# Adding the two expert sums into the residual: reloads and VectorE additions, or accumulating transfers issued by GpSimd

## What is computed

```python
    # hier_moe: every token goes to its two best experts
    y = jax.ops.segment_sum(y_buf[dest] * w_s[:, None].astype(h.dtype), tok_s, num_segments=n_tok)

    # first_block
        x = x + hier_moe(h, ...)
    return rmsnorm(x, norm_final)

    # second_block
    h = layer_norm(x, ln_in_g, ln_in_b)
    for l in range(DEPTH_2):
        proj = jnp.einsum('bsd,de->bse', h, w_in[l])
        ...
```

## Time and profile before

| | us |
|---|---|
| median of three runs | 2050.75 |
| lowest, highest | 2048.8, 2050.97 |
| the profiled execution, its own time | 2045.53 |
| span of its trace, first to last instruction | 2044.3 |
| of it: last expert product on TensorE ends | 757.5 |
| first product of the next layer starts | 801.3 |

### The profile page before, as it was taken

How to read it: one execution, slowest core, us unless ns; L and a number is a source line. 1 busy time by engine, 2 the same in 40 slices (tenths; PEclk the granted TensorE clock), 3 DMA queues, 4 the chain that set the end, 5 groups by cost and what they waited for, 6 DMA issues and landing times.

```text
span 2044.3 us, 26578 instructions
## 1 busy us (share of the span) xinstructions
PE 1842.1 (90%) x10396; PEld 1453.1 (71%) x10396; DVE 958.1 (47%) x1881; ACT 777.7 (38%) x1436; POOL 394.9 (19%) x438
## 2 busy tenths in 40 slices
PE   6999999986998762999899999998999899999997
PEld 5888776765554432876778888787876778888785
DVE  4358776554211015778445333233777445333234
ACT  3245476211333234566352232214566253232221
POOL 1019154102222211134002111000133002111001
PEclk9999999997999995998999999999998999999999
DMA  4334300474999983211222333232211222333231
GB/s 145 88 105 125 102 2 2 165 281 194 371 383 401 393 325 115 72 54 51 82 93 90 105 94 96 90 100 66 81 63 42 83 93 88 105 97 94 90 95 52
DMA packets 134884, 264.43 MB, mean 129 GB/s; under 512 B 11616, under 2 KB 92128, under 8 KB 122464
## 3 DMA queue, kind: packets, MB, share of 16 engines
q1 hardware_dynamic: 116320, 228.35, 32.6%
q10 hardware_dynamic: 13312, 25.90, 3.7%
q0 software_dynamic: 5120, 8.40, 1.3%
HBM read 254.22 MB, written 16.78 MB: 133 GB/s over the span
## 4 chain that ended last, share of the span: by engine, by line
PE 52%; DMA 9%; DVE 8%; ACT 3%; issue 2%; POOL 1%; PEld 1%; PEldq 0%; ACTq 0%; POOLq 0%; SPq 0%; DVEq 0%
PE b L507 15%; PE b L508 14%; PE b L509 14%; DMA m<-in_w_gate_up 6%; PE b L1987 3%; ACT m L620 2%; DVE m L2695 2%; DMA m<-in_w_down 1%; PE b L2520 1%; PE b L2012 1%; PE b L2502 1%; PE b L2488 1%; ACT m L688 1%; DVE m L692 1%; DMA s_h<-m 1%
## 5 line engine op out<-in xcount | busy, mean ns | idle before, releaser
L507 PE MATMUL b<-m,m 128*128 128x512 f32 (+3 forms) x2060 | 783.8, 380 | 62.6 <-DVE m L493 21.9
L509 PE MATMUL b<-m,m 128*128 128x512 f32 (+3 forms) x2060 | 773.9, 376 | 0.0
L508 PE MATMUL b<-m,m 128*128 128x512 f32 (+3 forms) x2060 | 773.8, 376 | 0.0
L493 DVE TENSOR_TENSOR m<-m,m 128x1024 fp32r<-128x1024 f32 (+1 forms) x212 | 278.3, 1319 | 514.3 <-ACT m L483 513.9
L507 PEld LDWEIGHTS b<-m,m 128*128 128x128 f32 x2060 | 394.1, 191 | 141.6 <-issue 36.9
L509 PEld LDWEIGHTS b<-m,m 128*128 128x128 f32 x2060 | 393.7, 191 | 67.1
L508 PEld LDWEIGHTS b<-m,m 128*128 128x128 f32 x2060 | 394.5, 191 | 64.1
L483 ACT ACTIVATE m<-m 128x1024 fp32r<-128x1024 f32 (+1 forms) x236 | 245.8, 1048 | 500.3 <-PE b L509 472.4
L2945 POOL TENSOR_TENSOR m<-m,m 128x512 fp32r<-128x512 f32 x44 | 71.1, 1636 | 422.1 <-ACT m L2891 422.1
L1987 PE MATMUL b<-m,m 128*64 128x256 f32 x1024 | 126.5, 390 | 26.9 <-DMA m<-in_w_gate_up 25.2
L1987 PEld LDWEIGHTS b<-m,m 128*64 128x64 f32 x1024 | 73.5, 139 | 78.2 <-issue 38.2
(11 more groups left out here) (339 smaller groups left out, 1895.8 us busy)
## 6 DMA issues: line engine op xcount, KB each, us to landing
m<-in_w_gate_up SPq DMA_DIRECT2D x64, 1024.0 KB
m<-in_w_gu SPq DMA_DIRECT2D x88, 512.0 KB, 3.6
m<-in_w_down SPq DMA_DIRECT2D x32, 1024.0 KB
m<-in_w_in SPq DMA_DIRECT2D x48, 512.0 KB, 3.8
m<-in_w_down SPq DMA_DIRECT2D x44, 512.0 KB, 3.7
m<-in_w_in SPq DMA_DIRECT2D x20, 448.0 KB, 3.6
m<-in_w_o SPq DMA_DIRECT2D x16, 512.0 KB, 4.0
s_gt<-m ACTq DMA_DIRECT2D x16, 256.0 KB, 2.0
```

The lines of the kernel that those rows point to most:

```text
L493: e.tensor_tensor(flat(wlo[HX[i]], i), flat(raw[RX[i][0]], i), fr(flat(whi[HX[i]], i)), ALU.subtract).then_inc(sem("w_lo"), 1)
L507: e.matmul(out, xh, yh, start=start, stop=False, skip_group_check=True)
L508: e.matmul(out, xh, yl, start=False, stop=False, skip_group_check=True)
L509: return e.matmul(out, xl, yh, start=False, stop=stop, skip_group_check=True)
```

## The change

The eight reloads and VectorE's eight additions go. GpSimd issues eight transfers that add into `X1` in SBUF: first those of the first half of `Y2` for the four tiles. For each tile it then waits until that one has landed (`yb` at 16), and issues the one of the second half. VectorE's multiplication and ScalarE's squares wait for `yb` at 32, both sums added. GpSimd's four roots stand behind the eight transfers. The other lines only place semaphore counts anew.

```diff
         def sync_final(e):
             e.wait_ge(*at("over", 1))
-            for t in range(NT):
-                e.dma_start(YA[2 * t + 1], Y2[S + t * P:S + t * P + P, :]).then_inc(sem(f"ya{2 * t + 1}"), 16)
...
         def scalar_final(e):
             e.drain().then_inc(sem("over"), 1)
-            for t in range(NT):
-                e.dma_start(YA[2 * t], Y2[t * P:t * P + P, :]).then_inc(sem(f"ya{2 * t}"), 16)
...
-                    e.wait_ge(*at("f_sum", i + 1))
+                    e.wait_ge(*at(f"yb{i}", 32))
                     e.wait_ge(*at("rms_sq", SQUARES[2] + i))
...
         def vector_final(e):
             for i in range(7):
                 if i < 4:
-                    x, y = YA[2 * i], YA[2 * i + 1]
-                    e.wait_ge(*at(f"ya{2 * i}", 16))
-                    e.wait_ge(*at(f"ya{2 * i + 1}", 16))
-                    e.tensor_tensor(x, x, y, ALU.add).then_inc(sem("f_pair"), 1)
-                    e.wait_ge(*at("f_pair", i + 1))
-                    e.tensor_tensor(X1[:, i, :], X1[:, i, :], x, ALU.add).then_inc(sem("f_sum"), 1)
+                    y = YA[2 * i + 1]
...
-                    e.wait_ge(*at("f_sum", i + 1))
+                    e.wait_ge(*at(f"yb{i}", 32))
...
         def gpsimd_final(e):
+            for t in range(NT):
+                e.dma_start(X1[:, t, :], Y2[t * P:t * P + P, :], accum_op=ALU.add).then_inc(sem(f"yb{t}"), 16)
+            for t in range(NT):
+                e.wait_ge(*at(f"yb{t}", 16))
+                e.dma_start(X1[:, t, :], Y2[S + t * P:S + t * P + P, :], accum_op=ALU.add).then_inc(sem(f"yb{t}"), 16)
             for t in range(NT):
                 ln_root(e, 0, t)
```

## The result

| | before | changed |
|---|---|---|
| median of the timed executions, us | 2050.97 (7; 2048.8 to 2056.06) | 2063.02 (7; 2055.49 to 2065.46) |
| ratio, with its 95% interval | | 1.0047 [1.0029, 1.0066] |
| that is, in us | | +9.6 (5.9 to 13.5) |
| the profiled execution, its own time | 2045.53 | 2063.7 |
| span of its trace | 2044.3 | 2062.5 |

The ratio is estimated from all executions of both kernels, whose means (2051.86 and 2061.58) are 9.7 us apart; the medians are 12.1 apart. The changed kernel is slower by 0.47%. The two traces lie 18.2 us apart, nearly twice the 9.6 us. So the first thing to do is to split them at two marks in code that the change leaves alone: the issue of the last scatter, and the first product. Between them lies the stage, 8.3 us longer. The other 9.9 us lie outside: 5.1 ahead of the last scatter and 4.8 behind the first product.

A forecast was written before the change was run, and what follows sets the result against it. Bound: the chain of waits from last scatter to TensorE's first product. A0 = 773.45 + 4.0 + 5 x 2.68 = 790.9, product at 810.4 instead of 801.26; 2050.75 + 9.1 = 2059.9 us, range 2048 to 2070.

The forecast's parts named there:

- A0: Time at which tile 0 holds both sums; forecast at 790.9 us, where the kernel before has 777.66.
- fixed part: GpSimd's transfers, issue to data flow: 2.35 us as for reloads plus 1.0 for GpSimd's own issue, 3.35 us.
- release: Last scatter's landing to GpSimd's first issue, past the branch: ScalarE's 2.78 us assumed, issue at 770.1.
- the weights ahead of A0: SyncE's next three weight chunks, 1.57 MB at 390 GB/s, put wholly ahead of tile 0's sums: 4.0 us.
- The gain: VectorE's dropped additions bring TensorE's first product to A0 + 19.5 in place of + 23.6: 4.1 us.
- Two passes per tile: Accumulating transfers read SBUF as well as DRAM: 2.68 us a tile, first product 9.1 us later; chance 0.45.
- One pass: Rival on accumulating transfers: second read overlaps the first, 1.34 us a tile, 2.4 us later, 2053.2; chance 0.20.
- the third pass: Rival on accumulating transfers: software queue's factor 1.5 too, 4.0 us a tile, 17.3 us later, 2068; three or more 0.22.
- The weights give way: Rival on SyncE's weights: they fall behind the sums; at one pass 1.6 us earlier, 2049.2; chance 0.08.
- The roots: Rival: transfers out of order make tile 0's root on GpSimd wait for the last issue; costs its lateness; no chance given.
- Faster: Rival: GpSimd leaves the branch without the 2.78 us, plain tile speed, ahead of weights; 4.5 us earlier, 2046.2; chance 0.05.
- From the product on: TensorE's first product to the end: same 1243.0 us as before; a change by some us would mean being wrong.

The follow-up runs named there:

- plain_hold: The changed kernel with its eight transfers made plain (sums left out) and SyncE's next weights held back until all have landed; stage 40.37 us, no ratio timed.
- hold: The changed kernel with SyncE's next weights held back until all eight sums are in; ratio to the kernel before 1.0024.
- order: The changed kernel with GpSimd's eight transfers issued in another order, tile 0's second sum fourth instead of fifth; ratio to the kernel before 1.0076.
- after_again: The changed kernel once more, unedited, under a new name; ratio to the kernel before 1.0046.
- early: The kernel before with all eight reloads issued by SyncE once the scatters have landed, without waiting for the branch; ratio to the kernel before 1.0007.
- hybrid: The kernel before with second sums added by GpSimd's transfers, first sums still reloaded by ScalarE and added by VectorE; ratio to the kernel before 1.0019.

## Why the prediction was right, point by point

It forecast 2059.9 us in a range of 2048 to 2070, slower with 0.64. The changed kernel takes 2063.02. The forecast was a shift of 9.1 us from the median of before; the two timed comparisons give 9.6 and 9.4. In the traces the way from the first issue to A0 was 0.8 us shorter than laid out. In that sum the tiles were 0.7 us too dear and the fixed part 0.6, while the weights were 0.55 too cheap, so part of the closeness is errors that cancel.

| step | predicted | measured |
|---|---|---|
| release: last scatter's landing to the first issue | 2.78 | 3.32 |
| fixed part of a chain of GpSimd's transfers | 3.35 | 2.7 accumulating (15.44 - 5 x 2.54), 3.6 plain (9.99 - 5 x 1.27) |
| the weights ahead of A0 | 4.0 | 4.55, alone 4.21 |
| one accumulating tile | 2.68 | 2.54 |
| first issue to A0 | 20.75 | 19.99 |
| A0 to the first product | 19.5 | 19.28 |
| period, with a wait for the root | 3.77, 0.66 | 3.81, 0.69 |
| the stage | + 9.1 | + 8.3, + 8.5 |

- **The gain** of 4.1 us came: 23.60 - 19.28 = 4.3. The layout by hand of three programs from the earlier trace rows was off by 0.2 us in 19.5, and that is its rounding: A0 + 8.8 with 3.3, 1.05 and 1.15 us makes + 14.3, not + 14.4, and 0.1 us was put on top. Kernels with four different A0 have 19.26 to 19.28 here.
- **Two passes per tile** was the step that decided. Its price held (2.54 us for 2.68); that the second read is what it pays for is not shown. One pass falls with `plain_hold` against `hold` (1.27 and 2.54), and so does the third pass: the factor of 1.5 of the software queue in the earlier trace rows doesn't hold for whole tiles. To take the row of another access pattern only as a bound was right.
- **The weights give way** fell. They cost about what the prediction said, but not in the way it said. They don't pass first. They delay the first landing by 2.9 us and slow each of the four tiles behind it by 0.4: 2.9 + 4 x 0.4 = 4.5. Of the mechanism only that two queues share the engines was right, so that the size came out is in part luck.
- **The roots** don't block in the changed kernel: the last issue is done at 793.6 (792.71 + 0.88) and GpSimd then idles 4.89 us. They do in `order`, where the wait decides. The prediction had called it a mishap of transfers out of order; a change of the issue order is enough.
- **Release** was 0.5 us short. Over the kernels that wait for the branch it goes from 10.45 to 11.36 us, and from 10.56 to 11.19 for the kernel before alone. Up to 0.9 us of a comparison of two stages may be this alone. The traces in which both engines issue show GpSimd's first issue beside ScalarE's: 0.08 us ahead in the changed kernel (775.41 against 775.49), 0.6 behind in `after_again` (779.67 against 779.06), 0.1 to 0.9 behind in the six others. So GpSimd does not leave the branch earlier, as the case *Faster* wanted, and mostly somewhat later.
- **From the product on** the prediction wanted the same 1243.0 us. The trace has 1247.8, which it had named as a sign of being wrong. The second trace of the kernel before has 1246.2, `early`, which runs the old code there, 1247.2, and `order` 1243.0. So the sign was set too sharply: this part differs by that much without the change. The mean clock of the execution alone doesn't order it (`early` has 0.959, `after_again` 1246.6 us at 0.953).

## What to carry to other kernels

An addition in a transfer isn't free: the tile takes twice the engines' time, and where the transfer already ends the wait, as here, that is paid almost in full (5.45 and 5.79 us for five tiles), while VectorE's addition had hidden a round trip and was worth only 4 of its 9.9 us. Before you give a chain of transfers to one queue, count how many tiles stand ahead of the one that is waited for, and what other queues issue at the time of its first. And split every pair of traces at marks outside the edit before you explain their difference: here half of it wasn't the change's.

## What the runs showed of the hardware that was not expected

- **Issuing costs more when it accumulates.** GpSimd's first four accumulating issues take 1008 to 1928 ns by the trace, plain ones 537 to 609; the later ones 867 to 876 against 537 to 540. Each is less than the 2.54 us in which a tile moves.
- **Transfers on another queue, issued at the same time, delay the first landing more than their share**: 8.2 us in place of 5.3 beside three weight chunks (8.9 where they went 0.66 us ahead). Later tiles lose 0.4 us each (0.2 there).
- **GpSimd's root of 128 numbers takes 0.55 us alone and 1.49 us where VectorE's additions run** (changed kernel; kernel before, and `hybrid`). Dropping the additions shortened the root by 0.9 us; the round trip that is now waited for is shorter than the one that they covered.
- **A large addition on GpSimd stops VectorE's next one**: 3.25 us in place of 1.23.
- **The same code outside the stage takes 2002 to 2015 us**, with a mean granted clock of 0.960 down to 0.953. A single trace can be up to 13 us from another without any edit to that code.
